# Recurrent stage of a mixed transformer: one multiply per level for keys and queries, decays by level halves, scores of both halves with the preceding head's sums

## The chip, the cores and the metric

The kernel runs on one core of a Trainium2 chip. Its time is the device time of one execution in microseconds; of several runs the median is given. The engines are PE (TensorE), DVE (VectorE), ACT (ScalarE), POOL (GpSimd) and SP (SyncE, which issues the DMA of the weights). In the rows of the profile PEld is the load of weights into PE, L12 is line 12 of the kernel, `ps` is PSUM (8 banks of 512 fp32 words in each partition).

## The reference, cut to what matters

Two transformer blocks of two layers each run one after the other on 256 tokens of width 1024, all in fp32. The change touches one stage of it, the recurrence of the second block's first layer (6 heads of width 128), which the reference computes chunk by chunk:

```python
def step(state, inp):
    q_, k_, v_, c_ = inp                       # c_ = running sum of log f in the chunk
    diff = c_[:, :, :, None, :] - c_[:, :, None, :, :]
    decay = jnp.exp(jnp.where(tri[:, :, None], diff, -jnp.inf))
    scores = jnp.einsum('bhtd,bhsd,bhtsd->bhts', q_, k_, decay)
    o = (jnp.einsum('bhts,bhsv->bhtv', scores, v_)
         + jnp.einsum('bhtd,bhdv->bhtv', q_ * jnp.exp(c_), state))
    ...
# in the layer: q = silu(q_raw), k = 1 - f, f = lb + (1 - lb) * sigmoid(f_raw), v = i_raw
o = hgrn2_recurrence(q, 1.0 - f, i_raw, jnp.log(f))
main = rms_norm_2(o, hgrn_o_gain) * jax.nn.silu(g_raw)
```

So an output row t of a head is the sum over s <= t of v_s times sum over d of q_t,d k_s,d exp(c_t,d - c_s,d). The stage also projects q, f, i, g (12 slots of weights of 256 columns) and the query of a small memory attention (1 slot).

## The kernel before, in words

The whole kernel is a stream of weight slots of 1 MB, each in a ring of four. SP loads a slot into `raw`; ACT rounds it to fp32r (`whi`, L1256); DVE subtracts to get the low part (`wlo`, L1875); PE multiplies with both parts (three products of 256 columns, or one of 512 and one of 256). All instructions of an engine are issued in one order that is written out by hand; semaphores join the engines. `filled[b]` counts how often PE filled PSUM bank b, `drained[b]` how often its reader emptied it, and `fill(b)` on PE waits until all earlier fillings of b are drained.

The recurrent stage (`kind == "hgrn"`) has 13 slots s = 0 to 12. Each slot is 8 k-tiles of 6 products, and after k-tiles 1, 3, 5 and 7 there is a hook (places p = 0 to 3), so 12 products lie between two hooks. The work of the heads is hung on these hooks by `hgrn_order(s)` and `head_work(z)`; every engine walks the same list. Head j has the items i = 0 to 5; head 0 begins with item 0 at the last hook of slot 3 and items 2 to 5 at slot 4's places 1, 2, 3 and slot 5's place 0; from there on every hook is one item: head 1 has its item 0 at slot 5, place 1, head 4's item 5 is at slot 11, place 0, and head 5 takes slot 11, place 1 to slot 12, place 2. The steps are:

- turn(j): PE transposes log f of the head into bank 2 (L1043), ACT takes the high part (`hlh`, L1643), DVE the low part (`hll`, L2388), which drains bank 2.
- decay(j, t), t = the half of the tokens: PE multiplies the turned log f with constant 0/1 matrices `hseg` for 8 levels into banks 4 and 5 (L1055, L1056), ACT takes the exponential into `hD` (L1650), DVE multiplies with the keys into `hxk` (L2400) and with the queries in place (L2402). Level n splits the tokens into segments of 2^n; only the keys of left segments and the queries of right ones are used.
- scores(j, t): 15 small products of 64 columns into bank 6 + t (L1071, L1072), and with t = 1 the product of the two halves in bank 3 (L1076, "cross"). DVE masks (L2410), adds the seven levels (L2416) and copies (L2409, L2414, L2419) into `hdiag`, `hrect`, `hcross`.
- sums(j): five products with the values `hnat` (L1086, L1087, L1089) into bank 3 (bank 6 for the last head); ACT copies and squares them.
- norm(pair): PE adds the squares of two heads over the partitions (L1097), ACT takes the root; DVE scales in `normed` (L2431).

Before, item 0 is decay(j, 0), item 2 decay(j, 1) and sums(j-1), item 3 scores(j, 0) (for heads 2 and 4 also a norm), item 4 turn(j+1), item 5 scores(j, 1). Between the heads' items DVE and ACT have the slots' own work in the same queue: DVE's split L1875 at the place that `split_at` names, the slot's result (L2496, L2498, L2492), the gates (L2448, L2453, L2459), and ACT's L1256, sigmoid and tanh (L1710).

The memory attention (`unit_steps`, two units) runs inside slots 3 to 5. Its last part, `end(3)`, is at slot 5, place 1, ahead of the head's item there: PE puts unit 1's output into bank 2 (L748), ACT copies it (L1385), and DVE's L2028 (`lower_part`) drains the bank.

After the stage the slots of kind `out` multiply `yh`, k-tiles in the order 6, 7, 0 to 5; ahead of k-tile 0 PE runs the last norm.

Of the kernel before, what the change touches and what calls it, by code (L numbers as in the profile page):

```python
# [115 lines left out]
def mixed_transformer(nc, A, C, out):  # L116
# [99 lines left out]
    with ExitStack() as ctx:  # L216
# [79 lines left out]
        hq = at("hq", 0, [P, 6, SEQ])  # L296
        hk = at("hk", 6 * K, [P, 6, SEQ])
# [4 lines left out]
        hD = at("hD", 28 * K, [P, 2, 8, P])  # L302
        hxk = at("hxk", 36 * K, [P, 2, 8, P])
# [8 lines left out]
        hmul = at("hmul", 66 * K, [P, 7 * HD])  # L312
# [240 lines left out]
        def _(pe):  # L553
# [220 lines left out]
            for kind, *arg in PLAN:  # L774
# [258 lines left out]
                elif kind == "hgrn":  # L1033
                    e0 = n.e
                    turn_fill = {}

                    def head(what, hh, t):
# [9 lines left out]
                        elif what == "decay":  # L1047
                            pe.wait_ge(drained[2], turn_fill[hh])
                            pe.wait_ge(seg_ready, 1)
                            hi, lo = hlh[:, hh % 2, t, :], hll[:, hh % 2, t, :]  # L1050
                            whole = hseg[:, 8 * P:] if t else hseg[:, 7 * P:8 * P]

                            def decays(dst, rhs):

                                mm(dst, hi, rhs, start=True, stop=False)  # L1055
                                return mm(dst, lo, rhs, start=False, stop=True)  # L1056

                            fill(4)
                            decays(ps[:, 4, :], hseg[:, 0:512]).then_inc(filled[4], 1)
                            fill(5)  # L1060
                            decays(ps[:, 5, 0:3 * P], hseg[:, 512:7 * P])
                            decays(ps[:, 5, 3 * P:], whole).then_inc(filled[5], 1)
                        elif what == "scores":
                            pe.wait_ge(hx_ready, 2 * hh + t + 1)
                            fill(6 + t)
                            for lv in range(7):
                                for b in (0, HD):
                                    k_, q_ = hxk[:, t, lv, b:b + HD], hD[:, t, lv, b:b + HD]
                                    if lv == 6:
                                        k_, q_ = hk[:, hh, t * P + b:t * P + b + HD], hq[:, hh, t * P + b:t * P + b + HD]  # L1070
                                    mm(ps[b:b + HD, 6 + t, lv * HD:(lv + 1) * HD], k_, q_, start=True, stop=True)  # L1071
                            mm(ps[0:HD, 6 + t, 7 * HD:], hxk[:, t, 6, 0:HD], hD[:, t, 6, HD:], start=True, stop=True)\  # L1072
                                .then_inc(filled[6 + t], 1)
                            if t:
                                fill(3)
                                mm(ps[:, 3, 0:P], hxk[:, 0, 7, :], hD[:, 1, 7, :], start=True, stop=True).then_inc(filled[3], 1)  # L1076
                        elif what == "sums":

                            pe.wait_ge(summed, e0 + 3 * (hh // 2) + 3)
                            pe.wait_ge(hs_ready, hh + 1)  # L1080
                            b = sums_bank(hh)
                            fill(b)
                            for t in range(TT):
# [4 lines left out]
                                if t:  # L1088
                                    last = mm(o, i0, hcross[:, :], start=False, stop=True, skip_group_check=True)  # L1089
# [1613 lines left out]
```

## Time and profile before

| | |
|---|---|
| median of 3 runs | 2307.98 us (2307.56 to 2308.77) |
| time of the profiled execution | 2307.86 us, of which its span 2306.1 us |
| PE / PEld busy | 99% / 87% |
| DVE / ACT busy | 73% / 57% |
| DMA | 178 GB/s from HBM over the span |
| PE's granted clock | 1.00 of full in the whole span |
| the recurrent stage | about 1465 to 1590 us of the span |

Matmuls overlap in the rows: a product of 256 columns shows about 280 ns, but starts 118 ns after the one ahead of it. So the starts are what counts on PE. On DVE an instruction that waits for nothing starts some 0.08 us before the one ahead of it ends. Idle time stands in brackets with what ended it.

### The profile page before, as it was taken

Reading aid. Unit: us, or ns where it says so; the run is one execution under the profiler, and the core shown is the slowest. Engines: PE = TensorE matmul, PEld = TensorE weight load, DVE = VectorE, ACT = ScalarE, POOL = GpSimd, SP = SyncE. Lnnn points to the kernel's source line nnn. Section 1 sums busy time; section 2 is a strip of 40 time slices with the busy share of each in tenths; the row PEclk is TensorE's granted clock in tenths of the full one; section 3 lists DMA queues with packets and bytes.
Section 4 is the critical chain, followed back from the end, with each engine's and each line's share of the span. In section 5 each row is a group of like instructions: output and inputs, shape, how many; then the busy total and the mean of one; then the engine's idle time right before and its main releaser. Section 6 shows DMA issues by size and latency. Waiting matters only on the chain.

```text
span 2306.1 us, 36238 instructions
## 1 busy us (share of the span) xinstructions
PE 2289.7 (99%) x14223; PEld 1999.9 (87%) x14223; DVE 1686.4 (73%) x2119; ACT 1315.6 (57%) x1623; POOL 67.5 (3%) x104
## 2 busy tenths in 40 slices
PE   8999999999999999999999999999999999999999
PEld 7888888988888888889888888988888888889888
DVE  6876678787667666778775776699776677777773
ACT  7554566565455455665654664655654565467552
POOL 2100111000000001000000000000000000000000
PEclk9999999999999999999999999999999999999999
DMA  7655655565556556545655565523565555644563
GB/s 244 195 182 190 186 156 177 165 197 186 183 189 193 183 183 185 162 158 174 204 189 183 184 192 188 165 93 128 187 188 194 184 183 189 219 131 147 185 195 130
DMA packets 344898, 411.92 MB, mean 179 GB/s; under 512 B 7764, under 2 KB 291878, under 8 KB 344656
## 3 DMA queue, kind: packets, MB, share of 16 engines
q1 hardware_dynamic: 340384, 399.30, 54.0%
q0 software_dynamic: 4176, 10.95, 1.8%
q8 instruction: 81, 1.33, 0.2%
q14 instruction: 33, 0.27, 0.0%
q10 hardware_dynamic: 224, 0.07, 0.0%
HBM read 409.08 MB, written 1.21 MB: 178 GB/s over the span
## 4 chain that ended last, share of the span: by engine, by line
PE 96%; DVE 1%; ACT 1%; issue 0%; DMA 0%; SPq 0%; ACTq 0%; DVEq 0%
PE ps L589 53%; PE ps L592 26%; PE ps L617 1%; PE ps L618 1%; PE ps L619 1%; PE ps L633 1%; PE ps L635 1%; PE ps L634 1%; PE ps L731 1%; PE ps L748 1%; PE ps L966 1%; PE ps L967 1%; PE ps L968 1%; PE ps L766 1%; PE ps L1071 0%; ACT whi L1256 0%
## 5 line engine op out<-in xcount | busy, mean ns | idle before, releaser
L589 PE MATMUL ps<-h,whi 128*128 128x512 f32 x3552 | 1122.7, 397 | 0.0
L1875 DVE TENSOR_TENSOR wlo<-raw,whi 128x2048 fp32r<-128x2048 f32 x377 | 863.5, 2291 | 261.0 <-ACT whi L1256 259.8
L1256 ACT ACTIVATE whi<-raw 128x2048 fp32r<-128x2048 f32 x377 | 721.5, 1916 | 248.2 <-DMA raw<-in_ffn_w_down 159.8
L592 PEld LDWEIGHTS ps<-h,wlo 128*128 128x128 f32 x3552 | 666.3, 188 | 161.8
L592 PE MATMUL ps<-h,wlo 128*128 128x256 f32 x3552 | 702.6, 279 | 0.0
L589 PEld LDWEIGHTS ps<-h,whi 128*128 128x128 f32 x3552 | 538.9, 188 | 10.2 <-issue 9.8
L589 PE MATMUL ps<-act,whi 128*128 128x512 f32 x1408 | 444.8, 396 | 0.0
L1299 ACT ACTIVATE accT<-ps 128x512 f32<-128x512 f32 x227 | 135.5, 597 | 393.3 <-PE ps L592 393.0
L592 PEld LDWEIGHTS ps<-act,wlo 128*128 128x128 f32 x1408 | 264.7, 188 | 65.4
L592 PE MATMUL ps<-act,wlo 128*128 128x256 f32 x1408 | 278.3, 278 | 0.0
L1884 DVE TENSOR_TENSOR accT<-ps,accT 128x512 f32<-128x512 f32 x200 | 138.1, 691 | 167.5 <-ACT accT L1299 166.0
L589 PEld LDWEIGHTS ps<-act,whi 128*128 128x128 f32 x1408 | 212.3, 188 | 0.0
L1890 DVE TENSOR_TENSOR accT<-accT,rstd 128x512 f32<-128x512 f32 x200 | 140.7, 704 | 8.0 <-ACT rstd L1274 1.2
L1282 ACT ACTIVATE h<-xT,cols 128x256 fp32r<-128x256 f32 x96 | 43.3, 502 | 85.2 <-DVE xT L2235 51.7
L1489 ACT ACTIVATE act<-accT 128x512 f32 (+1 forms) x88 | 55.7, 633 | 48.6 <-DVE accT L2159 48.6
L617 PE MATMUL ps<-h,whi 128*128 128x256 f32 x272 | 82.6, 304 | 0.0
L618 PE MATMUL ps<-h,whi 128*128 128x256 f32 x272 | 76.6, 282 | 0.0
L619 PE MATMUL ps<-h,wlo 128*128 128x256 f32 x272 | 76.1, 280 | 0.0
L1977 DVE CUSTOM_DVE_ANT_0 Lmix<-ps,biasr 128x256 f32<-128x256 f32 x96 | 35.6, 420 | 49.1 <-PE ps L731 49.1
L2159 DVE TENSOR_TENSOR accT<-accT 128x512 f32<-128x512 f32 x88 | 61.0, 693 | 10.1
L1368 ACT ACTIVATE Lmix<-Lmix,negm 128x256 f32<-128x256 f32 x96 | 47.6, 497 | 23.8 <-DVE negm L1977 23.8
L2163 DVE TENSOR_TENSOR act<-accT,act 128x512 f32 (+1 forms) x88 | 61.0, 693 | 0.0
(393 smaller groups left out, 2348.8 us busy)
## 6 DMA issues: line engine op xcount, KB each, us to landing
raw<-in_ffn_w_gate SPq DMA_DIRECT2D x88, 1024.0 KB, 5.3
raw<-in_ffn_w_up SPq DMA_DIRECT2D x88, 1024.0 KB, 5.3
raw<-in_ffn_w_down SPq DMA_DIRECT2D x88, 1024.0 KB, 5.0
raw<-in_w_in SPq DMA_DIRECT2D x30, 1024.0 KB, 5.5
raw<-in_w_gate SPq DMA_DIRECT2D x24, 1024.0 KB, 5.6
raw<-in_w_in_a SPq DMA_DIRECT2D x13, 1024.0 KB, 5.3
raw<-in_w_branch SPq DMA_DIRECT2D x12, 1024.0 KB, 5.0
raw<-in_w_o SPq DMA_DIRECT2D x8, 1024.0 KB, 5.1
```

The costliest lines, as they stand in the source:

```text
L589: mm(dst, whi[:, r, col:col + P], rhs, start=first, stop=False, skip_group_check=True)
L592: return mm(dst[:, 0:SEQ], wlo[:, r, col:col + P], rhs[:, 0:SEQ], start=False, stop=last, skip_group_check=True)
L617: mm(dst, whi[:, g % RING, w], rhs[:, k, 0:SEQ], start=first, stop=False, skip_group_check=True)
L618: mm(dst, whi[:, g % RING, w], rhs[:, k, SEQ:], start=False, stop=False, skip_group_check=True)
L619: last = mm(dst, wlo[:, g % RING, w], rhs[:, k, 0:SEQ], start=False, stop=k == ends[1], skip_group_check=True)
L1256: fn(whi[:, gr % RING, :], raw[:, gr % RING, :], ACT.Copy).then_inc(hi_done, 1)
L1299: fn(accT[:, c % 2, :, :], ps[:, b:b + 2, SEQ:], ACT.Copy).then_inc(acc_copied, 1)
L1875: v.tensor_tensor(wlo[:, gr % RING, :], raw[:, gr % RING, :], whi[:, gr % RING, :].bitcast(F32), ALU.subtract)\
L1884: v.tensor_tensor(dst, acc(er), accT[:, (c if cr is None else cr) % 2], ALU.add).then_inc(summed, 1)
L1890: v.tensor_tensor(dst, dst, rstd2 if root is None else root, ALU.mult).then_inc(acc_free, 1)
L2159: v.tensor_tensor(b1, b0, b1, ALU.mult).then_inc(prod_ready, 1)
L2163: v.tensor_tensor(a_t[:, :, SEQ:], b1, a_t[:, :, 0:SEQ].bitcast(F32), ALU.subtract).then_inc(act_lo, 1)
```

## The change

`hD` and `hxk` become one buffer `hX` for each of two heads, [level, 256 tokens]. The exponentials go there, and DVE does one multiply per level in place, over all 256 tokens, in which the second operand takes keys in left segments and queries in right ones (`hk` and `hq` now lie in one tile). decay(j, 0) makes levels 0 to 3 of both halves, decay(j, 1) levels 4 to 7. The scores of both halves are one item, behind the sums of the head before, and DVE handles both halves with one instruction each. The cross product goes into bank 2, as a step of its own. The sums' five products are in another order. The norms, `normed` and DVE's splits move to other places. In the diff the parts of PE come first, then those of DVE.

```diff
+        before = [("sums", j - 1, 0)] if j else []
         if j == HEADS:
-            return [("sums", j - 1, 0), LAST_NORM] if i == 0 else []
-        w = {0: [("decay", j, 0)], 1: [], 2: [("decay", j, 1), ("sums", j - 1, 0)], 3: [("scores", j, 0)],
-             4: [("turn", j + 1, 0)], 5: [("scores", j, 1)]}[i]
-        if j == HEADS - 1 and i >= 4:
-            w = [("scores", j, 1)] if i == 4 else []
-        if i == 2 and j == 0:
-            w = w[:1]
-        if i == 3 and j in (2, 4):
-            w = w + [("norm", j // 2 - 1, 0)]
-        return w
+            return before + [LAST_NORM] if i == 0 else []
+        if i == 0:
+            return ([("cross", j - 1, 0)] if j else []) + [("decay", j, 0)]
+        if i == 1:
+            return [("norm", (j - 3) // 2, 0)] if j in (3, 5) else []
+        if i == 2:
+            return [("decay", j, 1)]
+        if j == HEADS - 1:
+            return {3: before + [("scores", j, (0,))], 4: [("scores", j, (1,)), ("cross", j, 0)], 5: []}[i]
+        return {3: [], 4: [("turn", j + 1, 0)], 5: before + [("scores", j, (0, 1))]}[i]
...
-        hq = at("hq", 0, [P, 6, SEQ])
-        hk = at("hk", 6 * K, [P, 6, SEQ])
+        hkq = at("hkq", 0, [P, 2, 6, SEQ])
+        hk, hq = hkq[:, 0], hkq[:, 1]
...
-        hD = at("hD", 28 * K, [P, 2, 8, P])
-        hxk = at("hxk", 36 * K, [P, 2, 8, P])
+        hX = at("hX", 28 * K, [P, 2, 8, SEQ])
...
                         elif what == "decay":
...
-                            fill(4)
-                            decays(ps[:, 4, :], hseg[:, 0:512]).then_inc(filled[4], 1)
-                            fill(5)
-                            decays(ps[:, 5, 0:3 * P], hseg[:, 512:7 * P])
-                            decays(ps[:, 5, 3 * P:], whole).then_inc(filled[5], 1)
+                            for t_ in range(TT):
+                                fill(4 + t_)
+                                if t == 0:
+                                    last = decays(ps[:, 4 + t_, :], t_, hseg[:, 0:512])
+                                else:
+                                    decays(ps[:, 4 + t_, 0:3 * P], t_, hseg[:, 512:7 * P])
+                                    last = decays(ps[:, 4 + t_, 3 * P:], t_, hseg[:, (7 + t_) * P:(8 + t_) * P])
+                                last.then_inc(filled[4 + t_], 1)
...
                         elif what == "scores":
-                            pe.wait_ge(hx_ready, 2 * hh + t + 1)
+                                pe.wait_ge(hx_ready, 2 * hh + 2)
...
+                        elif what == "cross":
+                            pe.wait_ge(hx_ready, 2 * hh + 2)
+                            fill(2)
+                            mm(ps[:, 2, SEQ:SEQ + P], hX[:, hh % 2, 7, 0:P], hX[:, hh % 2, 7, P:], start=True, stop=True)\
+                                .then_inc(filled[2], 1)
+                            cross_fill[hh] = n.fill[2]
...
                         elif what == "sums":
...
+                            pe.wait_ge(drained[2], cross_fill[hh])
+                            mm(outs[1], rows_[0], hcross[:, :], start=True, stop=False, skip_group_check=True)
                             for t in range(TT):
-                                mm(o[:, 0:HD], i_[0:HD], hdiag[0:HD, t, :], start=t == 0, stop=t == 0, skip_group_check=True)
-                                last = mm(o[:, HD:], i_, hrect[:, t, :], start=False, stop=t == 0, skip_group_check=True)
-                                if t:
-                                    last = mm(o, i0, hcross[:, :], start=False, stop=True, skip_group_check=True)
+                                mm(outs[t][:, HD:], rows_[t], hrect[:, t, :], start=False, stop=True, skip_group_check=True)
+                            for t in range(TT):
+                                last = mm(outs[t][:, 0:HD], rows_[t][0:HD], hdiag[0:HD, t, :], start=False, stop=True,
+                                          skip_group_check=True)
...
                         elif what == "decay":
...
-                            m = 7 if t else 8
-                            link(v.tensor_tensor(hxk[:, t, 0:m, :], hD[:, t, 0:m, :], over(kt, m), ALU.mult))
-                            m = 8 if t else 7
-                            v.tensor_tensor(hD[:, t, 0:m, :], hD[:, t, 0:m, :], over(qt, m), ALU.mult).then_inc(hx_ready, 1)
+                            flat = hk[:, hh, :]
+                            for lv in range(4 * t, 4 * t + 4):
+                                w = 1 << lv
+                                d = hX[:, hh % 2, lv, :].rearrange("p (b s j) -> p b s j", s=2, j=w)
+                                kq = bass.AP(flat.tensor, flat.offset, [flat.ap[0], [2 * w, P // w], [6 * SEQ + w, 2], [1, w]])
+                                ins = v.tensor_tensor(d, d, kq, ALU.mult)
+                            ins.then_inc(hx_ready, 1)
...
                         elif what == "scores":
...
+                            a, m, top = t[0], len(t), 6 + t[-1]
...
+                            v.tensor_copy(hrect[0:HD, a:a + m, :], ps[0:HD, 6 + a:6 + a + m, 7 * HD:])
...
+                            v.tensor_tensor(hmul[:, a:a + m, :], ps[:, 6 + a:6 + a + m, 0:7 * HD], mask, ALU.mult).then_inc(drained[6 + a], 1)
...
+                            ins = v.tensor_reduce(hdiag[:, a:a + m, :], hmul[:, a:a + m, :].rearrange("p t (l n) -> p t n l", l=7), AX_X, ALU.add)
...
+                            last = v.tensor_copy(hrect[HD:, a:a + m, :], hdiag[HD:, a:a + m, :])
...
+                        elif what == "cross":
+                            n.use(2)
+                            dve.wait_ge(filled[2], n.fill[2])
+                            v.tensor_copy(hcross[:, :], ps[:, 2, SEQ:SEQ + P]).then_inc(drained[2], 1)
...
-                        if p == (3 if s < 6 or s % 3 == 0 else 1) and s > 1:
+                        if p == (3 if s < 6 else 0 if s % 3 == 0 else 2) and s > 1:
...
-                        if s in (7, 10):
-                            normed((s - 7) // 3)
+                        if s in (8, 11):
+                            normed((s - 8) // 3)
```

## Rows read from the trace of the kernel before

**Rows 1.** The page: parts 1 and 4

```profile
PE 2289.7 (99%) x14223; PEld 1999.9 (87%) x14223; DVE 1686.4 (73%) x2119; ACT 1315.6 (57%) x1623; POOL 67.5 (3%) x104
...
PE 96%; DVE 1%; ACT 1%; issue 0%; DMA 0%; SPq 0%; ACTq 0%; DVEq 0%
```

**Rows 2.** Windows of 10 us: busy time, clock, DMA

```profile
1500.00:1510.00 10.00, 8.64 (x92) 7.13 (x90) 7.99 (x18) 4.16 (x7) 0.00 (x0) 1.00 0.34 107
...
1560.00:1570.00 10.00, 10.00 (x94) 8.96 (x94) 9.81 (x12) 7.22 (x9) 0.00 (x0) 1.00 0.19 66
```

**Rows 3.** Timeline of PE (start us, us, line, operation) near the first head

```profile
1507.44 0.49 PE L1076 MATMUL ps<-hD,hxk 128*128 128x128 f32 x2 [1.00 <-ACT PTh L1342]
...
1510.30 0.50 PE L1055 MATMUL ps<-hseg,hlh 128*128 128x512 f32 x1
```

**Rows 4.** Timeline of PE: blocks of scores and of sums

```profile
1549.69 0.28 PE L619 MATMUL ps<-h,wlo 128*128 128x256 f32 x1
1549.98 0.92 PE L1071 MATMUL ps<-hD,hxk 128*64 128x64 f32 x24
...
1551.28 0.28 PE L618 MATMUL ps<-h,whi 128*128 128x256 f32 x1
...
1561.87 0.27 PE L1056 MATMUL ps<-hseg,hll 128*128 128x128 f32 x1
1562.07 0.43 PE L1086 MATMUL ps<-hdiag,hnat 64*128 64x64 f32 x2
...
1563.16 0.43 PE L1087 MATMUL ps<-hrect,hnat 128*128 128x64 f32 x2
1563.43 0.44 PE L1089 MATMUL ps<-hcross,hnat 128*128 128x128 f32 x2
...
1563.83 0.28 PE L618 MATMUL ps<-h,whi 128*128 128x256 f32 x1
```

**Rows 5.** Groups of DVE in the stage (busy us, mean ns of one)

```profile
L2416 DVE TENSOR_REDUCE hdiag<-hmul 128x64 f32<-128x448 f32 x12 | 11.4, 949 | 0.2
L2402 DVE TENSOR_TENSOR hD<-hD,hq 128x1024 f32<-128x1024 f32 x6 | 7.3, 1224 | 0.2
...
L2410 DVE TENSOR_TENSOR hmul<-ps,hmask 128x448 f32<-128x448 f32 x12 | 7.3, 607 | 0.0
L2402 DVE TENSOR_TENSOR hD<-hD,hq 128x896 f32<-128x896 f32 x6 | 6.6, 1092 | 0.2
```

**Rows 6.** Timeline of DVE where the stage's first head begins

```profile
1495.59 1.23 DVE L2400 TENSOR_TENSOR hxk<-hD,hk 128x1024 f32<-128x1024 f32 x1 [0.45 <-ACT hD L1650]
...
1497.86 2.28 DVE L1875 TENSOR_TENSOR wlo<-raw,whi 128x2048 fp32r<-128x2048 f32 x1
...
1505.55 0.69 DVE L2498 TENSOR_TENSOR accT<-ps,rstd 128x512 f32<-128x512 f32 x1
...
1510.36 2.28 DVE L1875 TENSOR_TENSOR wlo<-raw,whi 128x2048 fp32r<-128x2048 f32 x1
...
1514.63 0.42 DVE L2028 TENSOR_TENSOR yh<-ps,yh 128x256 fp32r<-128x256 f32 x1
```

**Rows 7.** Timeline of ACT at the same place

```profile
1506.28 0.63 ACT L1710 ACTIVATE accT<-accT 128x512 f32<-128x512 f32 x1 [5.84 <-DVE accT L2498]
```

**Rows 8.** Timeline of DVE over the last head

```profile
1572.43 0.21 DVE L2409 COPY hrect<-ps 64x64 f32<-64x64 f32 x1
...
1580.29 0.68 DVE L2496 SCALAR_TENSOR_TENSOR accT<-ps,rstd 128x512 f32<-128x512 f32 x1
...
1587.36 0.69 DVE L2459 TENSOR_TENSOR yh<-sq,yh 128x512 fp32r<-128x512 f32 x1
```

**Rows 9.** Timeline of ACT over the last head

```profile
1582.06 3.70 ACT L1256 ACTIVATE whi<-raw 128x2048 fp32r<-128x2048 f32 x2
```

**Rows 10.** Timeline of PE: before the last head, and the last norm

```profile
1571.46 0.49 PE L1076 MATMUL ps<-hD,hxk 128*128 128x128 f32 x2
...
1591.76 1.12 PE L1097 MATMUL ps<-sq,cst 128*128 128x512 f32 x2
```

More of the change, by code:

```diff
@@ L1034, in _ @@
                     e0 = n.e
[L1035 removed]
+                    turn_fill, cross_fill, sums_fill = {}, {}, {}
                     def head(what, hh, t):
@@ L1049, in head @@
                             pe.wait_ge(seg_ready, 1)
[L1050 to L1056, printed above, removed]
-                            fill(4)
-                            decays(ps[:, 4, :], hseg[:, 0:512]).then_inc(filled[4], 1)
@@ new lines, in decays @@
+                            def decays(dst, t_, rhs):
+                                mm(dst, hlh[:, hh % 2, t_, :], rhs, start=True, stop=False)
+                                return mm(dst, hll[:, hh % 2, t_, :], rhs, start=False, stop=True)
+                            for t_ in range(TT):
[6 more added lines that the diff above has]
+                                last.then_inc(filled[4 + t_], 1)
+                        elif what == "scores":
+                            for t_ in t:
+                                pe.wait_ge(hx_ready, 2 * hh + 2)
+                                fill(6 + t_)
+                                for lv in range(7):
+                                    for b in (t_ * P, t_ * P + HD):
+                                        k_ = q_ = hX[:, hh % 2, lv, b:b + HD]
+                                        if lv == 6:
+                                            k_, q_ = hk[:, hh, b:b + HD], hq[:, hh, b:b + HD]
+                                        mm(ps[b - t_ * P:b - t_ * P + HD, 6 + t_, lv * HD:(lv + 1) * HD], k_, q_, start=True, stop=True)
+                                b = t_ * P
+                                mm(ps[0:HD, 6 + t_, 7 * HD:], hX[:, hh % 2, 6, b:b + HD], hX[:, hh % 2, 6, b + HD:b + P],
+                                   start=True, stop=True).then_inc(filled[6 + t_], 1)
+                        elif what == "cross":
[4 more added lines that the diff above has]
+                            cross_fill[hh] = n.fill[2]
@@ L1093, in head @@
                             b = norm_bank(hh)
-                            if hh == HEADS // 2 - 1:
-                                pe.wait_ge(drained[sums_bank(HEADS - 1)], n.fill[sums_bank(HEADS - 1)])
+                            b_, f_ = sums_fill[2 * hh + 1]
+                            pe.wait_ge(drained[b_], f_)
                             fill(b)
@@ L2421, in head @@
                                 last.then_inc(hs_ready, 1)
+                        elif what == "cross":
+                            n.use(2)
+                            dve.wait_ge(filled[2], n.fill[2])
+                            v.tensor_copy(hcross[:, :], ps[:, 2, SEQ:SEQ + P]).then_inc(drained[2], 1)
                         elif what == "sums":
-                            n.sums = n.use(sums_bank(hh))
+                            n.use(sums_bank(hh))
                         else:
@@ L2460, in y_lower @@
                             .then_inc(y_lo, 1)
-                    n.post0, n.sums = n.post, 0
+                    n.post0, n.half = n.post, 0
                     def split_at(s, p):
-                        if p == (3 if s < 6 or s % 3 == 0 else 1) and s > 1:
+                        if p == (3 if s < 6 else 0 if s % 3 == 0 else 2) and s > 1:
                             split(n.g + s + 2, n.g + s + 2)
```

59 lines of the change are left out of this document (20 added, 39 removed).

## The prediction

> **What bounds the kernel now.** I read the page first: PE is busy 99% of the span, and the chain that ended last lies on PE for 96% of it [rows 1]. So the kernel ends when PE's stream of products ends, and an edit is worth what it takes from that stream or adds to its waits. DVE is 73% busy over all, but the windows of the recurrent stage show it at 9.81 of 10 us, beside a PE without a gap at the full clock [rows 2]. Only where the stage's first head begins does PE fall short, 8.64 of 10 us [rows 2]. The stage is thus nearly balanced: PE decides in its middle, and DVE's queue, in which the heads' steps stand behind the splits of the weights, can decide at its ends. The timeline of PE has one wait of note, 1.00 us ahead of the cross product of head 0, which wants bank 3 while ACT still has to empty it [rows 3]; ACT is late there since its sigmoid waited 5.84 us for DVE's result of slot 4 [rows 7].
>
> **What PE saves or gets in another place.** The number of products, their sizes and the fp32r/fp32 kinds stay the same. Two things change in PE's own time.
>
> A block of scores that stands alone takes 1.59 us from the last product ahead of it to the second one behind it, less 0.24 for two ordinary steps of 0.118: 1.35 us [rows 4] (others of this kind take 1.27). Its 30 matmuls start some 31 to 34 ns apart (24 of them in 0.92 us [rows 4]), so they need 1.06; 0.2 is the way in and out of the 64-column shape. With both halves in one block this is paid once. That is 0.2 for each of the heads 1 to 4 (head 0 and 5 lie beside waits, below): -0.8.
>
> A block of sums takes 1.96 us, from the last decay product at 1561.87 to 1563.83, less one step [rows 4]. Its ten matmuls alternate between 64 and 128 rows. The product at 1563.16 is followed, in the same shape, after 0.27 us; the first one at 1562.07 and those between, at each of which the shape changes, take 0.36 (1562.07 to 1563.16 holds three of them) [rows 4]. A change of shape thus costs 0.1. Before there are four (on entry and three inside); the new order cross, rect, rect, diag, diag has one inside, and its exit is the scores' entry. -0.3 for each, four of them in the middle: -1.2. The bound below is no gain (if 0.36 is what a product of 64 columns with its own load takes), the bound above 1.6 per block, hardly possible.
> The Trainium skill, TensorEngine Tiling (Array Packing), section Key Properties, says that a change of the tiling mode drains the engine. By that rule the order of the sums is worth something, and the 0.27 against 0.36 agrees.
>
> Moved and not changed: norm(1) (two matmuls of 512 columns, 1.12 us of which some 0.06 overlap with what follows [rows 10]: 1.06; it was in head 4's item 3) and head 4's cross product (0.22) leave the middle and come into the last head. Middle of the stage, from decay(1, 0) to the end of head 4's scores: -0.8 - 1.2 - 1.06 - 0.22 = **-3.3 us**, if no new wait arises.
>
> **DVE's prices.** A multiply of 1024 words takes 1224 ns and one of 896 takes 1092 [rows 5]: 1.03 ns a word and some 160 fixed, of which 80 are hidden behind the next one that waits for nothing. Four multiplies a half of decays, of 256 words: 0.35 us each at that rate. This trace shows no multiply whose second operand jumps between two tiles. The bounds are the contiguous rate and that of the level sum, which reads 448 words that lie 64 apart: (949 - 160) / 448 = 1.76 ns a word [rows 5], or 0.53 us for 256. Level 0 jumps at every word, so I take 0.53; levels 3 to 7 go in runs of 8 to 128 and get 0.35; 1 and 2 lie between, I take 0.35. So levels 0 to 3 take 1.6 us and levels 4 to 7 1.4, where each half took 2.27 (1495.59 to 1497.86 [rows 6]). The masks of both halves, 896 words, take 1.1 us (607 + 467), the level sums 1.75, the two copies 0.45: **3.35 us** for scores in one piece, where it was twice 2.0. The cross copy is 0.25. DVE so gets about 2 us less work per head, 12 us in all, but PE doesn't wait for it in the middle, so that is worth nothing by itself.
> The Trainium skill, Vector Engine (DVE) Microarchitecture Reference, section Measured stream behaviour on trn2, gives the full rate to runs of two adjacent words or more and about 1.73 ns a word to hops at each word. The level sum's 1.76 agrees; by it level 1 and 2 are at the full rate.
>
> **The new wait at the first head.** The cross product now fills bank 2. At slot 5, place 1, the order on PE is the memory unit's output (also bank 2), cross(0), decay(1, 0). So cross(0) waits until DVE's L2028 has drained the output, and in DVE's queue L2028 stands behind scores(0) of the hook before, now with both halves. Before, decay(1, 0) asked only for the older turn and started at 1510.30 [rows 3], while L2028 ran at 1514.63 [rows 6] and nobody waited.
> DVE's queue, step by step: multiplies from 1495.59, 1.6 us instead of 2.27: 1497.2. From 1497.86 to 1505.55 stood the split, the memory unit's reciprocals and scaling, multiplies (2.27) and scores(0, 0) (2.0) [rows 6], so 3.4 for the first two: 1500.6; multiplies 1.4: 1502.0. Scores(0, 0) no longer stands here, so slot 4's result starts at 1502.0 instead of 1505.55 [rows 6]. ACT's sigmoid follows at 1502.8 instead of 1506.28 [rows 7], with all that hangs on it up to DVE's split at 1510.36 [rows 6]: 1506.9. Split 2.2: 1509.1. Scores(0) 3.35: 1512.4. L2028 0.42: cross(0) can start at 1512.9, decay(1, 0) at 1513.1. PE itself is there at about 1509.4: the memory unit's transposes, which wait for DVE's scaling in both cases, come 0.7 earlier, the wait of 1.00 us [rows 3] and the old cross (0.2) are gone, and the second half of the scores (1.06) has moved in behind. So it waits 3.5 us. Against 1510.30 that is **+2.8 us**. From below, if nothing waited, it would be -0.65 (1509.4 and the cross's 0.25); from above, if levels 1 to 7 too were at 0.53, +4.1.
>
> **The last head.** I count from S, the end of head 4's scores and cross (1571.71: L1076 at 1571.46 [rows 10] and 0.25 of its own). Before, DVE took the scores up at 1572.43 and was done with those of head 5 at 1587.36 (S + 15.65) [rows 8]; the last norm on PE started 4.4 us later at 1591.76 (S + 20.05) [rows 10]. In these 4.4 us stand gates, slot 12's result, tanh and ACT's copies of the sums, one behind the other.
> After, DVE from S: scores(4) 3.35, gates 1.35 and cross 0.25: 5.0; multiplies 1.6, split of slot 13 2.2: 8.8; result of slot 11 0.6 and multiplies 1.4: 10.8; `normed` 0.75: 11.5. Then comes, new at slot 12's place 0, the split of slot 14, ahead of scores(5, 0). It needs ACT's L1256, which follows tanh of slot 11's result: that was at 1582.06 [rows 9], 1.8 us behind 1580.29 [rows 8], so now about S + 10.8, and the high part is there at S + 12.7. Split 2.2: 14.9. Scores(5, 0) and (5, 1) 2.0 each, cross 0.25: 19.2. The last norm starts 4.4 later, at S + 23.6, instead of S + 20.05: **+3.6 us**. PE alone would be there at about S + 20.3 (+0.3); the sums' saving of heads 4 and 5 is lost in this wait. The out stage starts with full weights in both cases and moves as a whole.
>
> **Sum.** -3.3 + 2.8 + 3.6 = +3.1 us on the profiled execution's 2307.86 (span 2306.1 and 1.8 around it): 2311.0; the median of the runs shown is 0.1 higher, 2307.98, so I say 2311.0. What a measurement of this kernel can't tell from no change is 0.2%, 4.6 us; +3.1 is 0.13%.
>
> **Rivals.**
> 1. Forecast, both waits come and nearly cancel what PE saves: 2311.0, 0.50. Its own range is 2308.5 to 2313.
> 2. Slower: the shape changes on PE cost nothing that the new order gives back (the 0.36 is the short product's own time). Place: sums and scores of heads 0 to 4; price: 2.0 us of saving gone, +5.1, 2313.1. It decides from 1.5 us of it on. For it: the products behind a 64-column one also start late. Against: 0.27 and 0.36 in the same block. 0.25.
> 3. The jumping operand costs more than the row on all levels: +1.3 at the first head (seven levels by 0.18), and at the last head hidden in the 1.2 us in which DVE waits for ACT: 2312.3, 0.10.
> 4. The bank-2 wait doesn't hold PE up (DVE gets to L2028 before PE gets to cross): the first head gives -0.65 instead of +2.8, 2307.5. Against: DVE would have to be 3.5 us earlier. 0.08.
> 5. Neither wait: -3.3 - 0.65 + 0.3 = -3.65, 2304.2; faster by over 0.2% needs more than that, so the sums' order must be worth twice what I take. 0.07, of which I give 0.05 to faster.
>
> Cases 1, 3, 4 and part of 5 are no change, with the edges of 1 and 3 above 4.6 us: faster 0.05, same 0.66, slower 0.29. The range goes from rival 4 to above rival 2, 2306 to 2314.5.
>
> **What the changed profile would show.** Idle on PE ahead of the cross product in bank 2 (new line), 3 to 4 us, at about 1509, put down to DVE's L2028. One at the sums or the norm of head 5, 3 us in all, behind the split of slot 14. Multiplies of 128x256, level 0 near 610 ns as a row of its own, the others near 425 (ends 80 ns under the next). Level sums 128x128 from 128x896 near 1.73 us. Blocks of sums 1.4 us instead of 1.7. DVE busy some 12 us less. Wrong would make it: another reader of bank 2, a stall on PE in the middle (decay(2, 1) or (4, 1) has only some 0.5 us between the exponentials' end and PE), or a clock under 1.00.

## The result, and the profile after

The changed kernel takes 2312.82 us (median of 14 runs, 2311.39 to 2315.34), the kernel before 2308.52 in the same comparisons (14 runs, 2307.56 to 2310.68). The ratio is 1.0019, 95% interval [1.0012, 1.0026]: 4.3 us slower where 3.1 was forecast, and inside the range. The middle of the interval is also inside the 0.2% that the prediction called no change, but the whole interval lies above 1: a loss is shown, and its upper end is beyond 0.2%. The profiled execution took 2312.79 us, its span 2310.9.

The page of the changed kernel, parts 1 and 4, beside [rows 1]:

```profile
PE 2288.2 (99%) x14223; PEld 1999.6 (87%) x14223; DVE 1674.7 (72%) x2123; ACT 1313.8 (57%) x1622; POOL 68.6 (3%) x104
...
PE 95%; DVE 2%; ACT 2%; DMA 1%; issue 0%; SPq 0%; DVEq 0%; ACTq 0%
```

PE is busy for 1.5 us less and DVE for 11.7 us less, and yet the span is 4.8 us longer. So the added time is for the most part idle time of PE, which part 4 hints at: the chain leaves PE for DVE and ACT for 4% of the span, before for 2%.

To place it I measure the stage from its first `qn` product to the start of its last norm, both on PE: 1476.07 to 1591.76 before, 115.69 us; 1477.29 to 1596.12 after, 118.83. Of the 4.8 us, 3.14 are in the stage. 1.2 lie ahead of it, in code that the change doesn't touch, and 0.4 behind it. The part ahead varies from one execution to the next: in the profiles of this study, whose code is the same there, the stage starts between 1475.99 and 1478.43. It arises in the first 20 us of the kernel: the first product with the low part of the weights (L592) starts at 18.17 us before and at 19.39 after, 1.22 apart, and the stage starts 1457.90 us behind it in both. The changed kernel's times below are thus to be read with a shift of 1.2 us.

PE's waits over the stage (engine and line, what released it, us in total, times, longest); before there were two, 1.0 and 0.4 us:

```profile
PE ps L1080 <- DVE yh L2038: 3.5, 1, 3.5
PE ps L1093 <- DVE hcross L2436: 1.5, 1, 1.5
PE ps L589 <- DVE accT L2511: 1.0, 1, 1.0
PE ps L766 <- DVE Lh L2022: 0.8, 1, 0.8
PE ps L1073 <- DVE hX L2411: 0.5, 1, 0.5
```

The first is the cross product of head 0 behind the drain of bank 2, the second, third and fifth are the last head's. Where the first head begins, PE's timeline, with the line that answers to [rows 3]:

```profile
1509.30 1.09 PE L748 MATMUL ps<-PTh,memv 128*64 128x256 f32 x8
1513.88 0.77 PE L1080 MATMUL ps<-hX 128*128 128x128 f32 x2 [3.49 <-DVE yh L2038]
1514.30 0.77 PE L1053 MATMUL ps<-hseg,hlh 128*128 128x512 f32 x1
```

and DVE's queue in the same stretch, beside [rows 6]:

```profile
1496.80 1.51 DVE L2411 TENSOR_TENSOR hX<-hX,hkq 128x256 f32<-128x256 f32 x4 [0.45 <-ACT hX L1659]
...
1501.70 1.43 DVE L2411 TENSOR_TENSOR hX<-hX,hkq 128x256 f32<-128x256 f32 x4
...
1507.85 2.28 DVE L1885 TENSOR_TENSOR wlo<-raw,whi 128x2048 fp32r<-128x2048 f32 x1
...
1510.25 1.07 DVE L2420 TENSOR_TENSOR hmul<-ps,hmask 128x896 f32<-128x896 f32 x1
1511.36 1.66 DVE L2422 TENSOR_REDUCE hdiag<-hmul 128x128 f32<-128x896 f32 x1
...
1513.31 0.43 DVE L2038 TENSOR_TENSOR yh<-ps,yh 128x256 fp32r<-128x256 f32 x1
```

PE is through with the memory unit's output at 1510.4 and then stands still, while DVE works off the split and the scores of both halves ahead of the drain (L2038) that PE wants. Less the shift, the cross product starts at 1512.7 (forecast 1512.9) and decay(1, 0) at 1513.1 (forecast 1513.1).

What I had not expected stands behind that wait. PE's windows, 1 us each (busy time, count, granted clock, DMA share, GB/s):

```profile
1514.00:1515.00 1.00, 1.00 (x4) 0.50 0.00 0
1515.00:1516.00 1.00, 1.00 (x4) 0.50 0.00 0
1516.00:1517.00 1.00, 1.00 (x6) 0.56 0.00 0
1517.00:1518.00 1.00, 1.00 (x10) 1.00 0.00 0
```

Once PE has stood idle for 3.5 us, the granted clock is at 0.50, the lower of its two levels (1.2 of 2.4 GHz), for about 3 us of work. The products of 512 columns then start 0.42 us apart instead of 0.23. The first sums start 4.92 us later in the stage than in the kernel without this wait (first experiment, 47.65 against 42.73): 3.5 is the wait, 1.4 the clock.

One block of sums and scores in the middle of the stage, beside [rows 4]:

```profile
1539.48 0.38 PE L1093 MATMUL ps<-hcross,hnat 128*128 128x128 f32 x2
1539.70 0.56 PE L1095 MATMUL ps<-hrect,hnat 128*128 128x64 f32 x4
1540.18 0.66 PE L1097 MATMUL ps<-hdiag,hnat 64*128 64x64 f32 x4
1540.77 0.92 PE L1073 MATMUL ps<-hX 128*64 128x64 f32 x24
...
1543.00 0.28 PE L634 MATMUL ps<-wlo,h 128*128 128x256 f32 x1
```

Its products of each kind now stand together (x2, x4, x4 instead of x2 five times). The sums take 1.3 us to the first score, and the scores of both halves 2.1 to 1542.9. From the last product ahead of the block to the second behind it, less two ordinary steps, that is 3.4; before it was 1.7 for the sums and 1.27 to 1.35 for each half, 4.2 to 4.3. So sums and scores save 0.8 to 0.9 us a head where I had 0.5.

The last head, on DVE, beside [rows 8]:

```profile
1585.15 2.29 DVE L1885 TENSOR_TENSOR wlo<-raw,whi 128x2048 fp32r<-128x2048 f32 x1 [1.16 <-ACT whi L1265]
1587.36 0.21 DVE L2418 COPY hrect<-ps 64x64 f32<-64x64 f32 x1
...
1591.39 0.29 DVE L2436 COPY hcross<-ps 128x128 f32<-128x128 f32 x1
```

and on PE, beside [rows 10]:

```profile
1591.94 0.46 PE L1093 MATMUL ps<-hcross,hnat 128*128 128x128 f32 x2 [1.48 <-DVE hcross L2436]
...
1594.39 0.73 PE L589 MATMUL ps<-yh,whi 128*128 128x512 f32 x2 [1.01 <-DVE accT L2511]
...
1596.12 1.12 PE L1106 MATMUL ps<-sq,cst 128*128 128x512 f32 x2
```

The split of slot 14 waits 1.16 us for ACT with both halves of the last scores queued behind it, and the last norm starts 23.5 us behind the end of head 4's scores (forecast 23.6, before 20.05).

DVE's new groups over the stage (busy us, mean ns of one), beside [rows 5]:

```profile
L2411 DVE TENSOR_TENSOR hX<-hX,hkq 128x256 f32<-128x256 f32 x48 | 17.6, 428 | 6.1 <-ACT hX L1659 6.0
L2422 DVE TENSOR_REDUCE hdiag<-hmul 128x128 f32<-128x896 f32 x5 | 8.7, 1747 | 0.2
```

The multiply by level takes 410 ns at the shortest, 418 in the median, and 505 at level 0, the only one that stands out.

### The profile page after: what moved, and what is told of

The parts are those of the page before. It is cut to its first block, busy times and chain, and to the rows that moved or that the text cites. A ratio compares the mean times of both kernels' runs of the same rounds, so it can differ in the third digit from the quotient of the medians.

```text
span 2310.9 us, 36255 instructions
## 1 busy us (share of the span) xinstructions
PE 2288.2 (99%) x14223; PEld 1999.6 (87%) x14223; DVE 1674.7 (72%) x2123; ACT 1313.8 (57%) x1622; POOL 68.6 (3%) x104
## 4 chain that ended last, share of the span: by engine, by line
PE 95%; DVE 2%; ACT 2%; DMA 1%; issue 0%; SPq 0%; DVEq 0%; ACTq 0%
PE ps L589 53%; PE ps L592 26%; PE ps L617 1%; PE ps L618 1%; PE ps L619 1%; PE ps L633 1%; PE ps L635 1%; PE ps L634 1%; PE ps L731 1%; PE ps L748 1%; PE ps L966 1%; PE ps L967 1%; PE ps L968 1%; PE ps L766 1%; DVE wlo L1885 1%; ACT whi L1265 1%
## 5 line engine op out<-in xcount | busy, mean ns | idle before, releaser
L592 PEld LDWEIGHTS ps<-h,wlo 128*128 128x128 f32 x3552 | 666.3, 188 | 161.9
L592 PE MATMUL ps<-h,wlo 128*128 128x256 f32 x3552 | 702.7, 279 | 0.0
L592 PEld LDWEIGHTS ps<-act,wlo 128*128 128x128 f32 x1408 | 264.7, 188 | 65.7
L592 PE MATMUL ps<-act,wlo 128*128 128x256 f32 x1408 | 278.4, 278 | 0.0
```

Source lines behind the costliest of these rows:

```text
L592: return mm(dst[:, 0:SEQ], wlo[:, r, col:col + P], rhs[:, 0:SEQ], start=False, stop=last, skip_group_check=True)
```

## The experiments

Each was compared with the kernel before in five rounds on one chip, where nothing else is said. "Stage" is the length as measured above: 115.69 us before, 118.83 after.

### Head 0's cross product in another bank

```diff
+    def cross_bank(hh):
+        return 3 if hh == 0 else 2
...
-                            fill(2)
-                            mm(ps[:, 2, SEQ:SEQ + P], hX[:, hh % 2, 7, 0:P], ...
+                            c_ = cross_bank(hh)
+                            fill(c_)
+                            mm(ps[:, c_, SEQ:SEQ + P], hX[:, hh % 2, 7, 0:P], ...
```

> The changed kernel with head 0's cross product in bank 3 instead of bank 2; everything else stays. My theory: the 3.5 us for which PE waits at head 0's cross product come only from sharing bank 2 with the memory unit's output, which DVE drains late; and the granted clock of 0.50 for some 2.5 us behind that wait comes from the wait. Both go: PE reaches decay(1, 0) 3.5 us earlier, and 1.25 us of slow products are gone: 4.7 us less than the changed kernel, 2308.1, about the kernel before. No PE wait over 1 us before the last head, clock 1.00 there. Rival A, DVE's queue as such holds the first head back: the wait comes back at the next step (decay(1, 1) or the sums of head 0), and the gain is under 2 us. Rival B, the clock fell for another reason: the gain is 3.5 us and a stretch at 0.50 remains.

Measured: 2308.95 us (2306.25 to 2310.2) beside 2308.82, ratio 0.9999 [0.999, 1.0008]. The stage is 113.91 us, 4.92 less than after. The 3.5 us wait is gone, the cross product starts at 1509.97, and no stretch of the stage has a low clock. The wait is bank 2's: with it go all the 4.9 us, and no wait comes back at a later step of the first heads. In the profiles that is more than the stage's whole loss (3.14); in the medians it is 4.2 of 4.3 us. This is also rival 4's case made real. The prediction gave it -0.35 us against the kernel before (2307.5). The stage of this profile has -1.78, the median +0.1: most of these runs are slower than the profiled one (2307.09), and the last section of the experiments shows where.

### The split of slot 14 at its old end

```diff
-                        if p == (3 if s < 6 else 0 if s % 3 == 0 else 2) and s > 1:
+                        if p == (3 if s < 6 or s == 12 else 0 if s % 3 == 0 else 2) and s > 1:
```

> The changed kernel with DVE's split of slot 14 back at the last place of slot 12 (behind slot 12's result), instead of ahead of the scores of head 5. My theory: the last head is late by DVE's queue, 1.16 us of waiting for ACT's high part and 2.2 us of split ahead of the scores. They go from there: the last norm starts about 2.2 us earlier relative to the end of head 4's scores (21.3 us behind it instead of 23.5), the wait of 1.48 us at the last sums is gone; 2.2 us less than the changed kernel, 2310.6. Rival: it only moves, since the split then stands ahead of what the output stage needs (y_lower): less than 0.7 us gained and a new PE wait in the first k-tiles behind the norm.

Measured: 2310.99 us (2310.25 to 2311.34), ratio 1.0008 [0.9999, 1.0017]. Stage 116.88, 1.95 less than after. The wait at the last sums is gone, the one for slot 12's result is 0.7 instead of 1.0, and 0.5 for the multiplies of the last head stays. The last norm starts 21.5 us behind the end of head 4's scores (23.5 after, 20.05 before), so 1.4 us of the last head's loss are not this split's. The first head's wait and low clock are as they were.

### Both

> Both edits together. If the two waits are independent places on one PE path, the gains add: 4.7 + 2.2 = 6.9 us less than the changed kernel, 2305.9, which is 2.6 us (0.11%) less than the kernel before: what the new orders save on PE would then be seen. If what PE saves in the middle is only an effect of PE coming later than DVE (the stall at the first head paying for it), the gain is under 5 us and waits show up in the middle.

Measured: 2305.02 us (2304.61 to 2306.21) beside 2308.82, ratio 0.9984 [0.9975, 0.9993]. Stage 111.85: 6.98 less than after, 3.84 less than before. The waits that are left on PE in the stage:

```profile
PE ps L769 <- DVE Lh L2026: 0.8, 1, 0.8
PE ps L592 <- DVE accT L2516: 0.7, 1, 0.7
...
```

The two parts add up (4.92 + 1.95 = 6.87 of 6.98), so the waits were independent. It is the fastest version of all, and near to rival 5, neither wait. The forecast gave that -3.65 us, the stage shows -3.84 and the medians -3.8. That this agrees so well is luck in part: the last head costs 1.4 us here instead of the 0.3 of the forecast, and the middle gives about 1 us more.

### The sums' order alone, on the kernel before

```diff
+                            mm(outs[1], rows_[0], hcross[:, :], start=True, stop=False, ...)
                             for t in range(TT):
-                                mm(o[:, 0:HD], i_[0:HD], hdiag[0:HD, t, :], ...)
-                                last = mm(o[:, HD:], i_, hrect[:, t, :], ...)
-                                if t:
-                                    last = mm(o, i0, hcross[:, :], ...)
+                                mm(outs[t][:, HD:], rows_[t], hrect[:, t, :], ...)
+                            for t in range(TT):
+                                last = mm(outs[t][:, 0:HD], rows_[t][0:HD], hdiag[0:HD, t, :], ...)
```

> The kernel before with one part of the change: the five products of the sums in the order cross, rect, rect, diag, diag. My theory: each change of the products' shape costs PE time, and this order has one change inside instead of three and none on entry: a block takes 1.3 us instead of 1.7 to 1.8, 0.3 to 0.48 us less, in five of six heads on the path: 1.5 to 2.4 us less than the kernel before. Rival 2 of the prediction, the short product's own time: the block takes as long as before, 0 us.

Measured: 2308.67 us beside 2308.82, ratio 0.9999 [0.999, 1.0008]. Stage 115.64, 0.05 less than before: next to nothing arrives of the 1.5 us and more that were expected. Taken alone, this looks like rival 2. But the block itself is shorter, from the last decay product to the third ordinary one 1.79 us instead of 2.08, so 0.29 each, what the prediction had taken for it (0.3). The waits in the stage tell where it went:

```profile
PE ps L589 <- DVE accT L2497: 1.0, 1, 1.0
PE ps L1071 <- DVE hD L2403: 0.8, 1, 0.8
```

The kernel before has neither. PE arrives earlier and waits for DVE, for head 3's decays (0.76 us at 1551.17) and for the result of slot 12 (0.96 at 1591.19).

### The old sums' order in the changed kernel

The diff is the one above, turned round and made on the changed kernel.

> The changed kernel with the five products of the sums in the old order (64-row and 128-row products taking turns). My theory: with the lighter DVE queue of the changed kernel PE sets the pace in the middle, so there the order is worth its price on PE: blocks of 1.7 to 1.8 us instead of 1.3, times the four blocks between the first and the last head, 1.2 to 1.9 us more than the changed kernel (2314.0 to 2314.7); the sums of heads 4 and 5 lie beside waits of the last head. Rival: as in the kernel before, the order is worth nothing in the total, since DVE takes it back: 0 us.

Measured: 2316.83 us (2314.17 to 2317.56, six runs) beside 2308.18, ratio 1.0033 [1.0021, 1.0045]. Stage 121.93, 3.10 more than after. The block in PE's timeline:

```profile
1540.85 0.43 PE L1094 MATMUL ps<-hdiag,hnat 64*128 64x64 f32 x2
1541.21 0.43 PE L1095 MATMUL ps<-hrect,hnat 128*128 128x64 f32 x2
...
1542.21 0.44 PE L1097 MATMUL ps<-hcross,hnat 128*128 128x128 f32 x2
1542.58 0.92 PE L1073 MATMUL ps<-hX 128*64 128x64 f32 x24
```

1.73 us to the first score instead of 1.29. From one head's sums to the next (by their cross product) it is 15.04, 15.82, 15.04 and 12.77 us, where the changed kernel has 14.54, 15.29, 14.53 and 12.22: 2.1 us in four, 0.5 each. The sums of head 0 begin 0.1 us later in the stage than in the changed kernel. The other 1.0 lies between the last sums and the last norm, where this execution's granted clock is at 0.55 and 0.50 from 1596 to 1602; such a fall comes with the new order too (the ninth experiment, below). The median lies 2 us above what was expected; the stage's 3.1 and a part behind it under the same low clock are more than the order alone. So the order is worth 0.5 us a head where DVE leaves PE room, and rival 2 falls.

### DVE made heavier in the changed kernel

```diff
                             for lv in range(4 * t, 4 * t + 4):
...
+                            if 1 <= hh <= 3:
+                                link(v.tensor_tensor(hpad[:, :], hmask[:, :], hmask[:, :], ALU.mult))
```

> The changed kernel with one more DVE multiply of 448 words (0.65 us, its result unused) behind each half of the decays of heads 1 to 3, some 3.9 us more DVE work in the middle of the stage. My theory: DVE has some 15% to spare there, so the stage takes as long as before: 0 us, no new wait on PE. Rival: the exponentials' way from DVE's result over tanh to decay(2, 1), with half a microsecond of room, becomes late: up to 0.6 us more for head 2, and if DVE were the bound, 3.9 us more.

Measured: 2314.48 us (2311.63 to 2315.65), ratio 1.0025 [1.0016, 1.0034]. Between the sums of heads 0 to 4 it is 14.53, 15.29, 15.02 and 12.22 us: only the third grew, by 0.49, with a new wait of 0.4 us for ACT's exponentials, at decay(4, 1) and not at head 2 as the rival had it. The stage of this profile is 121.60, 2.77 more than after; 1.3 of it lie ahead of the first sums and 1.0 behind the last, both under a clock of 0.50 (1512 to 1518, and 1594 to 1600). So 0.65 us more of DVE in each half is hidden in five halves of six and costs 0.5 in one. The middle of the changed kernel has that much room and hardly more. Of the stage's 2.77 the clock has 2.3; that the median's +1.7 is mostly the clock's as well is likely, but not shown.

### Sums' order on the kernel before, DVE made lighter

PE has the edit of the fourth experiment; the diff shows what is added on DVE.

```diff
-                            v.tensor_reduce(hdiag[:, t, :], hmul[:, :].rearrange("p (l n) -> p n l", l=7), AX_X, ALU.add)\
+                            v.tensor_reduce(hdiag[:, t, :], hmul[:, 3 * HD:].rearrange("p (l n) -> p n l", l=4), AX_X, ALU.add)\
```

> The kernel before with the new order of the sums and a lighter DVE: the level sum adds four of the seven levels and leaves the three smallest out (0.33 us less for each half, 4 us in all; it gives another result for that reason). In the run of the new order alone PE's saving of 0.29 us per block came back as waits for DVE's multiplies (0.8 us) and result (1.0 us). My theory: DVE's queue is the second bound of the kernel before, a microsecond behind PE; with it lighter both waits go, and the saving is seen: 1.5 us less than the kernel before, and some 0.4 us more since the wait for bank 3 of head 0 gets shorter; 2306.6 to 2307.2. Rival: those waits have nothing to do with how much DVE works (order of the queue): they stay, 0 us.

Measured: 2306.09 us (2305.74 to 2307.22) beside 2308.18, ratio 0.9991 [0.9982, 1.0]. Stage 113.52, 2.17 less than before. The two waits for DVE that the order alone had brought are gone:

```profile
PE ps L1076 <- ACT PTh L1343: 0.7, 1, 0.7
PE ps L766 <- DVE Lh L2013: 0.4, 1, 0.4
```

A lighter DVE alone was not run. But the waits of the kernel before bound what it could give: of the 2.2 us, 0.3 is the wait for bank 3 of head 0 (0.7 instead of 1.0), which is DVE's load and not the order's. So the same edit on PE is worth nothing with DVE's queue as it was, and about 1.8 us with a lighter one, which is six blocks of 0.29. DVE is the second bound of the kernel before, right behind PE.

### A shorter wait at the first head

```diff
-                            ins = v.tensor_reduce(hdiag[:, a:a + m, :], hmul[:, a:a + m, :].rearrange("p t (l n) -> p t n l", l=7), AX_X, ALU.add)
+                            l0 = 4 if hh == 0 else 0
+                            ins = v.tensor_reduce(hdiag[:, a:a + m, :], hmul[:, a:a + m, l0 * HD:].rearrange("p t (l n) -> p t n l", l=7 - l0), AX_X, ALU.add)
```

> The changed kernel with a lighter level sum in head 0 alone: three of the seven levels, the four smallest are left out (1 us less for both halves; another result for that reason). It shortens PE's wait for bank 2 from 3.5 to 2.5 us. If PE's clock falls only behind the longer wait (it held through 1.5 us at the last sums), the granted clock stays 1.00 and 1.0 + 1.25 = 2.25 us are gained against the changed kernel: 2310.6. If it falls as well behind 2.5 us, only 1.0 us: 2311.8 and a stretch at 0.50 as before.

Measured: 2312.76 us (2310.28 to 2314.68), ratio 1.0017 [1.0008, 1.0026]; four runs lie at 2310.3 to 2310.9, seven at 2312.7 to 2314.7. The wait is 2.42 us, 1.07 less. PE's windows behind it:

```profile
1514.00:1516.00 2.00, 2.00 (x10) 0.73 0.00 0
1516.00:1518.00 2.00, 2.00 (x12) 0.50 0.00 0
1518.00:1520.00 2.00, 2.00 (x17) 0.91 0.00 0
```

The clock falls all the same, a little into the work behind the wait instead of with it. The first sums begin 0.93 us earlier than in the changed kernel, so the clock's price went from 1.4 to 1.6 and most of the 1.07 stood. Yet the stage is 118.89 us long, as after: 1.0 was lost between the last sums and the last norm, where this profile too shows 0.50 (1594 to 1600), and another 1.1 behind the norm than in the kernel with the other bank. In the median nothing of the shorter wait arrives (2312.76 beside 2312.82 for the changed kernel), and it fits neither of the two times that were expected.

### Two more executions, for the clock (one profile each)

These are the ninth and tenth experiment. The runs of the first one lay mostly at 2308.5 to 2309.4 us, but one at 2306.25. The profile that I had was of a short one (2307.09).

> The changed kernel with head 0's cross products in the other bank once more, one profile, to see where TensorE's granted clock lies low in a usual execution of it. If the runs at a mean clock of 0.998 (2308.5 to 2309.4 us against the 2306.25 us at 1.0) owe their 2 to 3 us to a fall of the clock behind the waits of the last head (1.5 and 1.0 us), the stretch from 1585 to 1600 us shows 0.5 to 0.6 for 2 to 5 us and the stage is 115 to 117 us long instead of 113.9. If the fall lies elsewhere, the stage keeps 113.9 us and another window shows it.

Measured: 2311.1 us, stage 114.90, and 1.5 us more behind it. PE's windows at the last head:

```profile
1590.00:1592.00 2.00, 1.40 (x4) 0.50 0.55 186
1592.00:1594.00 2.00, 2.00 (x7) 0.50 0.00 0
1594.00:1596.00 2.00, 2.00 (x5) 0.50 0.00 0
1596.00:1598.00 2.00, 2.00 (x12) 0.87 0.00 0
```

with the same waits ahead of them as in the short run:

```profile
1588.15 0.46 PE L1097 MATMUL ps<-hcross,hnat 128*128 128x128 f32 x2 [1.47 <-DVE hcross L2441]
...
1590.60 1.22 PE L592 MATMUL ps<-yh,whi 128*128 128x512 f32 x2 [1.01 <-DVE accT L2516]
```

So the clock can fall behind the waits of 1.5 and 1.0 us too, and does so in one execution and not in the other, with the same idle times. It cost 2.5 us here, 1.0 up to the norm and 1.5 behind it. Four profiles with two such waits show it (this one, the fifth, the sixth and the eighth experiment), two don't (the changed kernel, the first experiment).

> The changed kernel without either wait once more, one profile. Both theories expect a stage of 111.9 us, no window below 0.9 between 1500 and 1600 us, and a time of 2304.5 to 2306 us: without waits of over 1 us on TensorE there is nothing for the clock to fall behind.

Measured: 2305.14 us, stage 111.87, clock 1.00 in each window of 10 us from 1500 to 1520 and from 1580 to 1600. Without waits of over 1 us the clock stays up in the stage, in both profiles of this version.

## Why the prediction was right, step by step

**The first head** held: the place (cross(0) in bank 2 behind L2028's successor), the chain on DVE that leads there, and the size, 3.49 us of wait for 3.5 forecast and +2.8 us at decay(1, 0) for +2.8. The first experiment, which takes away only the bank, shows that it is this wait. Three small errors met in it: level 0's multiply costs 505 ns instead of 610, the other seven 410 to 418 instead of 425, and the cross product itself runs under the low clock, 0.4 us instead of 0.2.

**The last head** held: +3.5 us for +3.6, through the split of slot 14 that waits 1.16 us for ACT (forecast 1.2). The second experiment shows that the place of this split is worth 1.95 of it. The other 1.4 to 1.5 are norm(1) and head 4's cross product, which have moved in (0.85 and 0.22), and the waits of 0.5 and 0.7 us for DVE that stay without the split. PE's own +0.3 in the forecast was not reached by any run.

**The middle** was mis-sized. Forecast -3.3 us. Measured from decay(1, 0) to the end of head 4's scores: 61.4 us before, 58.3 after, with slow clock in it, and 57.1 in the first experiment at the full clock, so -4.3. The term at fault is the price of sums and scores: 0.8 to 0.9 us a head instead of 0.2 + 0.3. The old order costs 0.5 of it in the changed kernel (fifth experiment), where the block stands directly ahead of the scores; ahead of an ordinary product it costs the 0.3 that I had taken (fourth). The rest, 0.3 to 0.4, is the scores' merge, for which I had 0.2. Against that, norm(1) was worth 0.85 us and not 1.06, and the second half of the decays takes 1.14 to 1.27 us where it took 1.04, a term that the sum did not have. One reading was also off: from 1561.87 to 1563.83 are 1.96 us before the step is taken away, 1.84 with it.
The Trainium skill, TensorEngine Tiling (Array Packing), section Key Properties, says that a change of the tiling mode drains the engine. The trace agrees: the same ten products are 0.29 us shorter in the kernel before and 0.44 to 0.5 in the changed one, in an order with one change of rows inside instead of three. The order also changes which columns of the bank are written one behind the other, and no run separates the two.

**The clock** was missing from the sum: +1.4 us in the profiled run, 0.2 of it at the cross product and 1.2 in the middle's stretch. The prediction had named a clock under 1.00 among the signs that would make it wrong, without a price. It came, and the middle's -1.0 and the clock's +1.2 nearly cancel, so that the stage came out at +3.14 for +3.1. That agreement is luck: two terms of 1 us were wrong in opposite directions. The profiled times are 4.9 us apart, since 1.2 are added in the first 20 us, which the change does not touch, and 0.4 behind the stage. The medians are 4.3 apart, 1.2 more than forecast. Runs in which the clock falls at the last head as well can be some of this: the four slowest runs have the lowest mean clock (0.996), and without them the median would be 0.4 lower. The rest is open.

**"DVE's lighter work is worth nothing by itself"** was the weakest sentence. PE alone waits for nothing in the middle [rows 2], that much holds. But the fourth and the seventh experiment show that PE's savings can only be had because DVE's load fell as well: on the old queue the sums' order gives 0.05 us, on a lighter one about 1.8. The windows had hinted at it, with DVE at 9.81 of 10 us [rows 2]; after, the same window has 7.90.

**The rivals.** 2 (the shape changes save nothing) fell by the fifth experiment. 3 (jumping operand slow at all levels) fell by the multiplies' 410 to 418 ns at levels 1 to 7. 4 and 5 fell as forecasts, since both waits came; with both edits the kernel takes 2305.02 us.
The Trainium skill, Vector Engine (DVE) Microarchitecture Reference, section Measured stream behaviour on trn2, gives the full rate to runs of two adjacent words or more, and 1.73 ns a word where one source hops by 4 KiB at each word. The first half agrees with levels 1 to 7, at (418 - 160) / 256 = 1.01 ns a word. Level 0, where one source hops by some 6 KiB at each word, measured (505 - 160) / 256 = 1.35 ns, between the two rates, and the measurement decides.

What stays open: what decides whether the clock falls behind a short wait. Two executions of one kernel with the same waits of 1.5 and 1.0 us differ in it, and no experiment here separates them. The stage starts up to 2.4 us apart from one execution to the next, and 2.25 us of that are there within the first 21 us: PE's first product behind its wait for ACT's high part starts at 12.99 to 13.90, and the sixteen products of 512 columns from there take 5.2 to 6.6 us. Why they differ is not explained.

## What to carry to other kernels

A step that takes an accumulator bank inherits the place of that bank's drain in another engine's queue: before moving it, write down what stands ahead of the drain. When PE has no gap and a second engine is at 98% beside it, a saving on PE alone arrives as a wait, and has to be made together with one on the second engine (0.05 us against about 1.8 for the same edit here). Price a wait of PE of over 1 us at more than its length, since the clock may fall behind it (1.4 us on top of 3.5, 2.5 on top of 1.5 and 1.0).

## What the runs showed of the hardware that was not expected

TensorE's granted clock goes to its lower level (1.2 GHz, 0.50 in the windows) after the engine has stood idle. It did so in every profile with the wait of 3.5 or 2.4 us at the first head, for some 3 us of work behind it in the changed kernel and some 6 in the one with the heavier DVE, at a price of 1.4 to 2.7 us. The first and third experiment take this wait away, and the fall goes with it. Behind idle times of 1.5 and 1.0 us (in the fifth experiment 1.5 and 0.5) that follow one another closely it fell in four profiles of six, for some 6 us, at a price of 2.1 to 2.5 us; behind a single one of 0.7 to 1.0 us (the kernel before, the second, third and fourth experiment) it didn't. Added to the waits this makes them up to twice as dear. Near the start of the kernel PE waits 2.7 to 2.9 us for ACT, and the sixteen products of 512 columns behind it start 0.32 to 0.41 us apart on the mean, where 0.23 is the step at the full clock. The clock's rows show 0.50 there in four of the twelve profiles (the first, third, sixth and seventh experiment) and 1.00 in the others, which have slow products too, so at that place the clock's rows and the products' pace don't agree. It also spreads the runs: the changed kernel's 14 lie over 4 us, the version without waits within 1.6. In single runs without a profile only the mean clock is known (0.998 or 0.999 in the ten up to 2313.2 us, 0.996 in the four above 2314.7), so where it was low there is inferred.

An order of matmuls that alternates between 64 and 128 rows is slower than the same matmuls sorted, by 0.29 us for ten in one kernel and 0.44 to 0.5 in the other, where the block stands directly ahead of products of a third shape.
